# Charging ScalarE's table loads to the clocks that order side and main work

## Time and profile before

| | |
|---|---|
| median of 3 runs | 2743.39 us (2743.01 to 2744.7) |
| the profiled execution's own time | 2743.12 us |
| its span in the profile | 2741.3 us |
| TensorE busy | 2627.9 us |
| VectorE busy | 1765.3 us |
| ScalarE busy | 1156.3 us |
| table loads | 44 |

### The profile page before, as it was taken

How to read it: one execution, slowest core, us unless ns; L and a number is a source line. 1 busy time by engine, 2 the same in 40 slices (tenths; PEclk the granted TensorE clock), 3 DMA queues, 4 the chain that set the end, 5 groups by cost and what they waited for, 6 DMA issues and landing times.

```text
span 2741.3 us, 36022 instructions
## 1 busy us (share of the span) xinstructions
PE 2627.9 (96%) x14572; PEld 2102.9 (77%) x14572; DVE 1765.3 (64%) x3008; ACT 1156.3 (42%) x1906; POOL 246.8 (9%) x259
## 2 busy tenths in 40 slices
PE   4999889999999998999999999999999999999997
PEld 3877577888878676788887888777787888777776
DVE  7778658766677765878577547544536557545544
ACT  3243544333242454533234464344434464444432
POOL 0000000001200000002010031000100132000100
PEclk9999999999999999999999999999999999999999
DMA  7442024555442211455553322321322323221312
GB/s 265 139 150 92 30 78 164 173 172 167 153 129 65 65 60 52 148 177 184 195 184 106 113 66 68 97 85 51 100 72 87 102 64 95 81 87 56 100 62 77
DMA packets 256869, 302.53 MB, mean 110 GB/s; under 512 B 10176, under 2 KB 230464, under 8 KB 256704
## 3 DMA queue, kind: packets, MB, share of 16 engines
q1 hardware_dynamic: 239728, 237.10, 27.3%
q0 software_dynamic: 16688, 62.66, 7.1%
q10 hardware_dynamic: 288, 0.47, 0.1%
HBM read 289.97 MB, written 2.10 MB: 107 GB/s over the span
## 4 chain that ended last, share of the span: by engine, by line
PE 87%; DVE 9%; ACT 3%; issue 1%; DMA 0%; DVEq 0%; ACTq 0%; SPq 0%
PE ps L572 85%; PE ps L785 2%; DVE wl L1423 1%; DVE hl L1429 1%; DVE stage L1488 1%; DVE recat L1722 1%; DVE ca L1429 0%; DVE uv L1429 0%; DVE strewn L1488 0%; DVE recq L1423 0%; ACT hh L943 0%; DVE rawt L1429 0%; DVE reck L1423 0%; DVE nrm L1423 0%; ACT recat L943 0%
## 5 line engine op out<-in xcount | busy, mean ns | idle before, releaser
L572 PE MATMUL ps<-hh,wh 128*128 128x512 f32 x2208 | 887.7, 402 | 32.9 <-DVE hl L1429 17.7
L572 PE MATMUL ps<-hh,wl 128*128 128x512 f32 x2208 | 866.0, 392 | 0.0
L572 PE MATMUL ps<-hl,wh 128*128 128x512 f32 x2208 | 865.6, 392 | 0.0
L1423 DVE TENSOR_TENSOR wl<-raw,wh 128x2048 fp32r<-128x2048 f32 (+3 forms) x234 | 451.1, 1936 | 170.7 <-ACT wh L943 170.7
L572 PEld LDWEIGHTS ps<-hh,wh 128*128 128x128 f32 x2208 | 416.5, 189 | 154.6 <-issue 40.3
L572 PEld LDWEIGHTS ps<-hh,wl 128*128 128x128 f32 x2208 | 416.5, 189 | 91.2
L572 PEld LDWEIGHTS ps<-hl,wh 128*128 128x128 f32 x2208 | 417.0, 189 | 80.7
L943 ACT ACTIVATE wh<-raw 128x2048 fp32r<-128x2048 f32 (+3 forms) x234 | 370.0, 1591 | 201.4 <-PE ps L572 190.9
L572 PE MATMUL ps<-fh,wh 128*128 128x512 f32 x432 | 170.2, 394 | 0.0
L572 PE MATMUL ps<-fh,wl 128*128 128x512 f32 x432 | 168.1, 389 | 0.0
L572 PE MATMUL ps<-fl,wh 128*128 128x512 f32 x432 | 168.1, 389 | 0.0
(11 more groups left out here) (302 smaller groups left out, 3697.3 us busy)
## 6 DMA issues: line engine op xcount, KB each, us to landing
raw<-in_w_in SPq DMA_DIRECT2D x75, 1024.0 KB, 5.3
strewn<-in_w_ada POOLq DMA_DIRECT2D x104, 512.0 KB, 4.0
raw<-in_w_up SPq DMA_DIRECT2D x46, 1024.0 KB, 6.1
raw<-in_w_in SPq DMA_DIRECT2D x44, 512.0 KB, 4.9
raw<-in_w_out SPq DMA_DIRECT2D x16, 1024.0 KB, 5.2
raw<-in_w_down SPq DMA_DIRECT2D x16, 1024.0 KB, 6.8
raw<-in_w_ada SPq DMA_DIRECT2D x12, 1024.0 KB, 5.0
stage<-in_w_ada SPq DMA_DIRECT2D x8, 1024.0 KB, 11.4
```

The costliest lines, as they stand in the source:

```text
L572: return e.matmul(o, a, b, start=start, stop=stop, skip_group_check=True)
L1423: return e.tensor_tensor(o, a, b, op)
```

## The change

The running clocks learn of table loads. A new dictionary says which set each unit needs, the clocks remember which set they last saw, and a unit that needs another one has 1.28 us added to its first ScalarE step. No instruction is added or removed by this; only `weave` can place units in another order. What is asked of the chain lengths (`left`) does not include it.

```diff
+TABLES = {"zs": ("sigmoid",), "q": ("sigmoid",), "g": ("sigmoid",), "a": ("sigmoid",), "ln3": ("sigmoid",), "gate": ("exp",), "mg": ("exp",),
+          "sx": ("exp", "ln"), "c2": ("exp", "ln"), "rn": ("ln",), "ln2": ("ln",), "c1": ("ln",)}
+TABLE_US = 1.28
...
-        self.late, self.old = [], 0
+        self.late, self.old, self.functions = [], 0, None
...
         done = when
+        needs = TABLES.get(unit[0])
+        switch = TABLE_US if needs and self.functions not in needs else 0.0
+        if needs and self.functions not in needs:
+            self.functions = needs[0]
         for engine, us, counts in cost_of(unit):
+            if engine == "ACT":
+                us, switch = us + switch, 0.0
             when = self.clock[engine] = max(self.clock[engine], when) + us
```

## The result

The changed kernel takes 2776.98 us (median of 4 runs, 2775.99 to 2777.97), the kernel before 2743.87 in the same set. That is 33 us slower by the medians. The ratio, estimated from all runs and not quite the quotient of the medians, is 1.0113 with a 95% interval of 1.0086 to 1.0140, or 31 us (24 to 38). 2745.4 us was forecast, in a range of 2735 to 2755. The direction was right, the size wrong by more than ten times.

A forecast was written before the change was run, and what follows sets the result against it. TensorE was taken as the bound, busy 2627.9 of 2741.3 us, leaving its idle time and clock to win or lose. 2743.1 + 0 + 2.7 − 0.7 + 0 = 2745.1, plus 0.3 for the median: 2745.4 us, range 2735 to 2755.

The forecast's parts named there:

- While main work is left, its follower is then placed at most one part later: Where main work is left: a charged unit's follower slips at most one part, six matmuls, 1.36 us.
- term (1): Mixer stretches with plenty of main work: added ScalarE time hidden behind VectorE's clock; cost 0, bounds −1.4 to +1.4 us.
- cover: Mixer stretches with plenty of main work: VectorE's queue hides the charges; without it some ten could each move a follower.
- Term (2): Last main work, `g` of pairs 1 and 2: parts used earlier, missing later; +2.7 us, bounds 0 to 10.9.
- Term (3): Mixer stretches without main work: waits of 1.72 and 5.29 us might shrink by a swap; −0.7 us, bounds −8.2 to +3.8.
- The clock: Behind a long wait, matmuls run at the lower clock level, so a part there costs 1.2 us more.
- The second network: Its layers' charged first gates and `c1`: TensorE never waits around them; cost 0, bounds −0.5 to +1.4 us.
- Clocks already slow: Planner's clocks take 194 us in the first mixer, the chip 175.8; charging loads makes due times later than the truth.
- Loads, 44 give or take two: Whole kernel: the number of table loads should stay at 44, give or take two for sides that swap.
- the slower rival: Mixers' last main parts used up too soon, leaving less cover for the side-only end; 2749 to 2755 us, chance 0.24.

The follow-up runs named there:

- first1: The changed kernel with one single charge of 1.28 us, at the first `sx` of the second mixer; 2756.61 us, ratio 1.0047 to the kernel before.
- take3: Old list, second mixer: pair 1's last recurrence level, with `zs` of pair 2, moved behind four parts of `g` pair 0; 2754.03 us against 2743.19.
- late2: Old list, the second mixer's first `s2` and the `s1` it allows moved later, nothing planned anew; 2742.52 us against 2742.77.
- keep_a: The changed kernel with the logarithm and exponential table kept instead of asked for again, 50 loads to 38; 2766.52 us, ratio 1.0081 to the kernel before.
- keep_b: The old list with the logarithm and exponential table kept instead of asked for again, 44 loads to 32; 2745.46 us against 2743.19.
- best_keep: The changed kernel with a charge for each place (0.45, 0, 1.28, 0.75 us) and the logarithm and exponential table kept; 2736.44 us, ratio 0.9983 to the kernel before.

## Why the prediction was wrong

**The step that failed** is the sentence "While main work is left, its follower is then placed at most one part later", and with it the 0 of term (1). first1 is that sentence put to the test: one charge, and 13.8 us where it allowed 1.4. The step took each placement by itself. In `weave` a missed turn opens the way for the next main chunk, and `use` brings a weight split along, 2.3 us on VectorE. The prediction read VectorE's load (84.71 of 100 us in the first mixer, 72.02 in the second) as cover: the charge is hidden behind VectorE. It is no cover, since VectorE's queue is walked in the order of the list, and a unit that loses its place waits there for what was put ahead of it, even while the engine stands idle. Under first1 the clocks have 0.6 us turned into 6.4, and the trace has `sn` 4.2 us later behind 3.02 us in which VectorE was idle. All that follows is planned on top of that.

**Term (1), 0 with bounds ±1.4.** From `zs` of pair 0 to `zs` of pair 2 the second mixer took 988.15 − 795.33 = 192.8 us before and 1008.60 − 805.26 = 203.3 after: +10.5 in the stretch that was costed at nothing. take3 shows that such a delay of the last pair is paid in full; in five of its eight executions 5 us or more were lost again, at a lower clock.

**Term (2), +2.7 with a bound of 10.9.** The mechanism, main work used before the side-only end, is shown for the second mixer (three parts fewer at `zs` of pair 2; take3 has +10.8 from that alone). In the first mixer both lists have the same eight parts left, and it is not shown there. The bound counted charges times one part, and that product has no hold on a list that is planned anew. Behind `zs` of pair 2 the second mixer took 81.0 us before and 91.1 after, +10.1, half of it idle time and half busy; the first mixer as a whole took 9.9 more.

**Term (3), −0.7.** In the first mixer the wait of `ro` went from 5.29 to 4.13 us and that for `apad` went, small gains where one was forecast. That both would appear in the second mixer, 5.30 and 1.72 us, was not seen.

**The clock.** It was in the forecast only as 1.2 us for a part behind a wait. It is 16.3 of 34.0 us, about half, in the profiled execution of the changed kernel. Late2 shows that 10 us of this kind can stand in a single trace by chance; that all four executions of the changed kernel have 0.977 to 0.980 speaks against chance here.

**The second network, 0 with bounds to +1.4.** Measured +4.3 with its charges alone. The forecast was that TensorE never waits there; new waits appeared, 138 us behind the later of the two charged places of the last layer. Which of the two charges that bear on the last layer did it was not tried.

**Clocks already slow.** Given as a reason against a gain. With the two costs put right that the traces had shown to be off, the kernel is still 20 us slower, so it explains at most the other 13.

**Loads, 44 give or take two.** There are 50, and keep_a puts about 10 us on loads. With the slower rival a mechanism that acts in the second mixer had been named, with a chance of 0.24, and priced at a third of the whole loss. That the direction was forecast rightly owes nothing to the sum: its +2.7 us was for single parts.

**What stays open.** That the old list is one good draw among many is argued, not shown. For it: 0.10 us, a single charge, truer costs and the full charge all make the second mixer longer by 13 to 21 us, and no re-planned second mixer that was run came out shorter. Only a few lists were run. How the loss of a re-planned second mixer divides between main work used too soon and its four additional loads is known only roughly (take3 and keep_a); first1 without its four loads, and `sn` alone behind the split, were not run. The first mixer's 9.9 us have no cause that an experiment shows. Why the granted clock fell at the end of one mixer and held at another is shown side by side and not explained.

## What to carry to other kernels

An order made by a greedy planner is not a smooth function of its costs. Judge a change of a cost by the list that comes out, not by the charge times its count, and look at what each missed turn lets in ahead: a unit waits in its engine's queue for whatever took its place, whether that engine is full or not. On the list of this kernel even truer costs brought a loss, so try the hand edit of two units as well; it helps to tell whether the place matters or the re-planning. Ask for each part of main work ahead of the last serial chain what it hides, since here it delayed that chain by its full length (take3).

## What the runs showed of the hardware

Shortening waits does not always bring their length back. In keep_b 6.2 us of idle time went and 6.9 us of busy time came, for the same 14572 matmuls, and the granted clock was 0.980 or 0.981 in six of its ten executions, lower than in sixteen of the 17 of the kernel before. In best_keep the clock mostly held, and the kernel gained. The products at the end of a mixer ran at either level, sixteen in 1.09 us or in 1.98, and in the changed kernel's last 100 us of the second mixer the mean was 0.83 of full speed where the kernel before had 0.97. The long runs of projection matmuls did not change (887.7 and 886.6 us for 2208 of them); what the clock took, it took from the small products between waits.

Where an engine is idle in many short pieces, idle time alone is no measure of what an edit brings; busy time has to be read beside it, and not from a single trace. One and the same list (late2) took 2741 to 2744 us in eight executions, at 0.982 to 0.989, and 2754 in two, at 0.977 and 0.978; the trace of one of these has 10.3 us more busy time than the earlier trace rows and no loss by the median.
